# Down-projection weights as one 4 MB transfer per expert, gated values in groups of four columns

## What is computed

```
logits = xt @ w_router + b_router            # 32 experts, top 4 of them per token
gate   = softmax(top_val)
hu     = xb @ w_up[e] + b_up[e]              # 1024 -> 2048
x_glu  = min(hu[:, :1024], 7);  x_lin = clip(hu[:, 1024:], -7, 7)
act    = x_glu * sigmoid(1.702 * x_glu) * (x_lin + 1)
y      = act @ w_down[e] + b_down[e]         # 1024 -> 1024
out[token] += gate * y                       # then RMSNorm
```

## Time and profile before

| | us |
|---|---|
| median of 3 runs | 1251.53 |
| the three runs | 1251.39, 1251.53, 1255.16 |
| span of the profiled execution | 1248.5 |
| PE busy in it | 1169.1 (94%) |

### The profile page before, as it was taken

How to read it: one execution, slowest core, us unless ns; L and a number is a source line. 1 busy time by engine, 2 the same in 40 slices (tenths; PEclk the granted TensorE clock), 3 DMA queues, 4 the chain that set the end, 5 groups by cost and what they waited for, 6 DMA issues and landing times.

```text
span 1248.5 us, 17019 instructions
## 1 busy us (share of the span) xinstructions
PE 1169.1 (94%) x7215; PEld 604.2 (48%) x7216; DVE 445.6 (36%) x766; ACT 250.3 (20%) x353; POOL 15.9 (1%) x30
## 2 busy tenths in 40 slices
PE   9999999999999999899899989898989989899997
PEld 9998988888633343333333333333333333333332
DVE  5754546666532233222222222222322222222232
ACT  4544445544401010001000000000000001000012
POOL 2200000000000000000000000000000000000000
PEclk9999999999999999999999999999999999999999
DMA  9645333377999999999999999999999999999996
GB/s 296 219 169 186 135 135 135 135 277 282 371 417 425 431 431 427 430 430 429 431 433 427 431 430 429 430 430 434 433 428 431 433 427 431 435 427 432 421 428 278
DMA packets 50031, 456.98 MB, mean 366 GB/s; under 512 B 5988, under 2 KB 6136, under 8 KB 31400
## 3 DMA queue, kind: packets, MB, share of 16 engines
q1 hardware_dynamic: 49544, 455.09, 87.7%
q10 hardware_dynamic: 448, 1.32, 0.3%
HBM read 455.35 MB, written 1.05 MB: 366 GB/s over the span
## 4 chain that ended last, share of the span: by engine, by line
PE 59%; DMA 35%; DVE 2%; SPq 2%; ACT 1%; issue 1%; DVEq 0%
PE ps L1384 57%; DMA ring<-in_w_up_dram 22%; DMA arena<-in_w_up_dram 12%; PE ps L1891 1%; DMA ring<-in_w_in_dram 1%; ACT w_split L588 0%; SPq L397 0%; DVE w_split L892 0%; SPq L399 0%; PE ps L1777 0%; PE ps L1573 0%; SPq L414 0%; DVE arena L1062 0%; SPq L391 0%; PE ps L1680 0%
## 5 line engine op out<-in xcount | busy, mean ns | idle before, releaser
L1384 PE MATMUL ps<-ring,arena 128*64 128x512 f32 x2304 | 523.2, 608 | 50.9 <-DMA ring<-in_w_up_dram 50.9
L1384 PEld LDWEIGHTS ps<-ring,arena 128*64 128x64 f32 x2304 | 163.9, 140 | 378.8 <-issue 300.3
L1384 PE MATMUL ps<-arena 128*64 128x512 f32 (+3 forms) x920 | 202.7, 563 | 17.0 <-DMA arena<-in_w_up_dram 16.1
L1296 DVE TENSOR_SCALAR arena<-ps 128x512 f32<-128x512 f32 x32 | 22.1, 692 | 487.3 <-PE ps L1384 487.3
L892 DVE TENSOR_TENSOR w_split<-ring,w_split 128x2048 fp32r<-128x2048 f32 x48 | 109.8, 2291 | 108.4 <-ACT w_split L588 108.1
L1384 PEld LDWEIGHTS ps<-arena 128*64 128x64 f32 (+1 forms) x920 | 78.2, 149 | 128.4 <-issue 100.2
L796 ACT ACTIVATE arena<-arena 128x512 f32<-128x512 f32 x32 | 20.2, 631 | 552.6 <-DVE arena L1296 552.6
L1384 PE MATMUL ps<-w_split,x_split 128*128 128x512 f32 x528 | 123.5, 392 | 0.7 <-ACT arena L624 0.5
L1384 PEld LDWEIGHTS ps<-w_split,x_split 128*128 128x128 f32 x528 | 98.4, 188 | 21.8 <-issue 1.2
L588 ACT ACTIVATE w_split<-ring 128x2048 fp32r<-128x2048 f32 x47 | 89.6, 1911 | 70.7 <-PE ps L1384 62.5
L1384 PE MATMUL ps<-x_split,w_split 128*128 128x256 f32 x768 | 94.7, 284 | 0.1
(11 more groups left out here) (251 smaller groups left out, 624.8 us busy)
## 6 DMA issues: line engine op xcount, KB each, us to landing
ring<-in_w_up_dram SPq DMA_DIRECT2D x40, 4096.0 KB, 31.1
ring<-in_w_down_dram SPq DMA_DIRECT2D x46, 2048.0 KB, 30.2
arena<-in_w_up_dram SPq DMA_DIRECT2D x14, 4096.0 KB, 31.1
ring<-in_w_in_dram SPq DMA_DIRECT2D x17, 2048.0 KB, 7.8
arena<-in_w_down_dram SPq DMA_DIRECT2D x14, 2048.0 KB, 30.0
ring<-in_w_up_dram SPq DMA_DIRECT2D x12, 2048.0 KB, 23.1
arena<-in_w_up_dram SPq DMA_DIRECT2D x4, 2048.0 KB, 23.5
ring<-in_w_up_dram SPq DMA_DIRECT2D x8, 1024.0 KB, 8.7
```

Source lines behind the costliest of these rows:

```text
L1296: dve.tensor_scalar(glu_c, ps[bank][:, :], LIMIT, None, ALU.min).then_inc(glu_ok, 1)
L1384: return pe.matmul(dst, lhsT, rhs, start=start, stop=stop, skip_group_check=True)
```

## The change

The down weights of experts 1 to 30 are loaded as one 4 MB piece over a pair of places: partition p takes eight neighbouring rows, a run of 32 KB (`load_down_pair`). The piece waits for the second of the two places, and lands with one semaphore count. `down` waits for that count once, ahead of d = 0, where it waited for each half.

Place d of the pair now holds, on partition p, hidden rows 8p+4d to 8p+4d+3. The gated values must match, so the up matmuls and their bias read their 512 columns in groups of four, skipping every other group: half 0 takes columns 0-3, 8-11, 16-19, ..., half 1 the others (`hidden_half`). The count of matmuls, and every shape, stay. Expert 0 keeps the old columns and the old pieces. The last expert keeps its five pieces, with rows chosen to match.

```diff
-        def load_down(sp, e, d, n):
-            rows = w_down[0, bass.ds(e, 1), d * 512:d * 512 + 512, :]
-            sp.dma_start(chunk_at[n % PLACES], rows.rearrange("e (p s) n -> p (e s n)", s=4))\
+        def load_down_pair(sp, e, n):
+            rows = w_down[0, bass.ds(e, 1), :, :]
+            sp.dma_start(pair_at[n % PLACES // 2], rows.rearrange("e (p s) n -> p (e s n)", s=8))\
               .then_inc(chunk_in[n % PLACES], 16)
...
             def down_chunks(e, base, n):
-                for d in range(DOWN_CHUNKS):
-                    sp.wait_ge(chunk_used, base + (n + d - PLACES + 1))
-                    load_down(sp, e, d, n + d)
+                sp.wait_ge(chunk_used, base + (n + 1 - PLACES + 1))
+                load_down_pair(sp, e, n)
...
-                rows = w_down[0, E - 1, d * 512:d * 512 + 512, :].rearrange("(p s) n -> p s n", s=4)
+                rows = w_down[0, E - 1, :, :].rearrange("(p d s) n -> d p s n", d=DOWN_CHUNKS, s=4)[d]
...
+            def hidden_half(row, half):
+                return row.rearrange("p (q d s) -> p q d s", d=DOWN_CHUNKS, s=4)[:, :, half, :]
+
             def up_bias(m):
-                bias(0, m % UNROLL, 0)
-                bias(1, m % UNROLL, D)
+                for bank, first in ((0, 0), (1, D)):
+                    for half in range(2):
+                        mm(half_bank(bank, half), pickL[:, m % UNROLL, :], hidden_half(bias_p[:, first:first + D], half),
+                           True, False)
...
-                        col = (2 * s + side) * D + half * 512
-                        ins = mm(half_bank(banks[side], half), xin[:, m % 2, 2 * c + s, :], w[:, col:col + 512],
-                                 False, last_of_all)
+                        row = w[:, (2 * s + side) * D:(2 * s + side) * D + D]
+                        cols = row[:, half * 512:half * 512 + 512] if banks == FIRST_BANK else hidden_half(row, half)
+                        ins = mm(half_bank(banks[side], half), xin[:, m % 2, 2 * c + s, :], cols, False, last_of_all)
...
                 pe.wait_ge(actT_ok, i * UNROLL + (u + 1))
+                if not last:
+                    chunk_landed(i, first)
                 for d in range(DOWN_CHUNKS):
-                    def whole_landed():
-                        if d:
-                            odd_landed(i, first + d, last)
-                        else:
-                            chunk_landed(i, first)
-                    if not last:
-                        whole_landed()
```

More of the change, by code:

```diff
@@ L329, in layer @@
         pair_at = [at(G0, 2 * CHUNK)] + [ring[:, 2 * n:2 * n + 2, :].rearrange("p a n -> p (a n)") for n in range(3)]
-        ODD_LANDED = {1: 2, 3: 3, 5: 3, 7: 2}
         def load_up_pair(sp, e, c, n):
@@ L1793, in chunk_landed @@
                 pe.wait_ge(chunk_in[n % PLACES], i * (16 * TURN_CHUNKS // PLACES) + 16 * (n // PLACES + 1))
-            def odd_landed(i, n, last):
-                pe.wait_ge(chunk_in[n % PLACES], i * 16 + 16 * (ODD_LANDED[n % PLACES] + int(last)))
             def up_part(i, m, n, c, s, banks, last_of_all):
@@ L1876, in down @@
                             pe.wait_ge(early_in[2 + d], 32)
-                        if last and k == 2:
-                            whole_landed()
+                        if last and k == 2 and d == 0:
+                            chunk_landed(i, first)
+                        if last and k == 2 and d == 1:
+                            pe.wait_ge(chunk_in[PLACES - 1], 32)
                         if last and d == 1 and k == 3:
```

## The result

| | median | runs | profiled span | end of the last down matmuls |
|---|---|---|---|---|
| before | 1251.89 | 1250.60 to 1255.16 (6) | 1248.5 | 1239.44 |
| changed | 1254.83 | 1253.92 to 1257.12 (6) | 1252.7 | 1243.58 |

The ratio is 1.0028, 95% interval 1.0015 to 1.0041: the change costs 2.9 us by the medians, 4.2 us between the two profiled executions, where 1.5 us was forecast.

The account below looks back on a forecast made before the run. DMA was taken to bound the experts, with DMA and PE both critical at the end. Landings -3.3 us and the last turn's wait +4.8 us net +1.5 us on 1251.5, giving 1253.0, range 1249.5 to 1256.5.

Parts of the forecast that it names:

- Part 4: Down matmuls of experts 29 and 30: PE waits for one 4 MB landing instead of two, +4.8 us.
- Part 1: Down weights of 30 experts: runs of 32 KB instead of 16 KB bring landings 3.3 us earlier, 0.11 us per expert.
- Part 2: Up matmuls and their bias: reading columns in groups of four costs 0 us.
- Rival D: Up matmuls: the gaps slow them beyond PE's cover, 87 us over 30 experts, 1339; chance 4%.
- the factor 1.47: Up matmuls: far-end slowdown from gaps, taken from weight loads of one float per 16 bytes (209 against 142 ns).
- Part 3: Issue of the 4 MB piece, 3.4 us later, thinnest at expert 1: costs 0, bound 0 to 2 us.
- Rival C: Expert 1: the DMA queue runs dry for up to 2 us as the piece comes late, 1253 to 1255; chance 8%.
- A: Last turn: no late wait, so the gain of the longer runs comes through whole, 1248.2; chance 8%.
- B: Down weight loads: 32 KB runs bring nothing and the late wait stays, 1256.3; chance 10%.
- E: Down weight loads: each transfer has a fixed price and 30 fewer save it, 3.85 us; 1% for anything beyond.

Follow-up runs that it names:

- the second set: The changed kernel once more, unedited, against the kernel before (1250.73): 1254.76, ratio 1.003 (1.0020 to 1.0041).
- The first set of runs: The kernel before with both 2 MB down pieces issued when the later place is free, first measurement: 1252.93, ratio 1.0008 (0.9999 to 1.0018).

## Why the prediction was right, and where it was not

The median of 1254.83 lies inside the range of 1249.5 to 1256.5, 1.8 us above the forecast; the rise is 2.9 us instead of 1.5, and 4.0 us in the second set. Two pieces of luck made it look closer than it was. The base was the median of three runs, one of them at 1255.16, and was put 3.0 us above the profiled span, where every run on record lies 1.8 to 2.0 us above its own; that lifted the forecast by 1.1 us. And the six runs of before beside the first result have a median of 1251.89, 1.2 us above that of the 29 runs beside the second. In spans, which have neither, 1250.0 was forecast and 1252.7 and 1252.3 were measured.

**Part 4, the late wait: right, in place and size.** The step forecast a wait of 2.7 us at expert 29; the profile has 2.73, the second 1.70. Arrival and landing were both put 2.5 to 2.6 us too early (1192.9 and 1195.6 against 1195.53 and 1198.12), by the same wrong gain in landings, which cancels in their difference. The price of +4.8 us is 4.7 by undoing it and 4.6 (span) to 5.2 (medians) by adding it to the kernel before. The forecast wait of 1.8 us at expert 30 is 2.44 in one profile and 0 in the other; in the latter the lower clock used up that time. PE started 0.1 us after the landing in both, where 0.05 was taken, and the 16.04 us behind it were 16.04 again. Steady state stayed covered, by 0.5 us as said: PE starts the down matmuls of most experts 0.7 us after their landing, where it starts 0.1 us after it when it waits, and no wait for down weights shows elsewhere.

**Part 1, the gain of the runs: the term that was mis-sized.** Landings of expert 30 came 0.7 us earlier in the profiled pair (1227.45 against 1228.15), 1.1 in the second, not 3.3. By the version without the late wait the whole term is worth 0.7 us in the median. The step turned a gain in bytes per us into 0.11 us per expert and took 30 of them off every later landing. Two things were wrong with that. The gain per expert is 0.08 us (0.076 to 0.081 by the mean of the counts), which is 0.9 us less over 30. It lies within the bounds that the step gave (0.056 to 0.128), and their plain mean, 0.092, is nearer to it than the weight of three to one was. And PE waits for the last of sixteen counts, which the step let move with the rest. At expert 30's landing the mean came 1.9 us earlier in the changed kernel's profile and 2.0 us in the second, but the last hung 3.3 and 3.0 us behind it, against 2.1 us before: 1.2 and 0.9 us of the gain did not reach PE. The rest, 0.3 to 0.4 us, is mostly that both profiles were 0.2 to 0.3 us behind before's at 387 us already. Whether that larger lag of the last count belongs to the change or to these executions is open.

**Part 2, the groups: right.** 7.03 us as before, and 1.0002 alone. Rival D is out, and so is the factor 1.47: a matmul that reads four floats of every eight pays nothing here. This is what the Trainium skill has in "SBUF — State Buffer", "Door 1: The DMA port swizzle", for lines of 16 bytes, and the 7.03 us agree with it for a matmul's moving operand too. The row of 195 ns in the earlier trace rows mixes 16 loads from `h_sb` without gaps, 192 ns, with the 32 of the gather, 196 ns; by either reading two floats per 16 bytes cost 2 to 3%.

**Part 3, the later issue: right at 0.** Rival C's mechanism is refuted by the run that does it alone (447.15 against 447.10). A delay of its size is there, in its place, but in the last count alone, without the shift of the mean that a queue run dry would bring. The first set of runs, with its late start, would have passed for C's proof.

**Rivals.** A (no late wait, 1248.2) is refuted by the two waits. B (runs bring nothing, 1256.3) is nearer to the net than the forecast was, but not its mechanism: runs of 8 KB cost 4.2 us. E (a price per transfer) has nothing left to explain: the same run has before's number of transfers and pays 9 ns for each run that an engine has more, and at that price the 8 runs fewer per expert are worth 0.07 of the 0.08 us. The fixed 2.0 us that the Trainium skill has in "DMA: Bandwidth & Descriptors", "Anatomy of one DMA — SWDGE (gpsimd) path", is not seen between the transfers of this queue: 30 fewer, and the last landing moved by 0.7 us. **The sum** was +4.8 - 3.3 = +1.5; measured it is +4.7 - 0.7 = +4.0 in the second set of runs, which is 1254.76 - 1250.73.

## What to carry to other kernels

A larger transfer is a later first byte for its reader. Before merging pieces, list every place where the reader arrives between the two old landings: in the steady loop the slack may cover them (0.5 us did here), at the end of the stream nothing does, so keep the last pieces small. Where waits in a chain are held by one landing, removing an earlier one gives nothing, and can make the last wait long enough for TensorE's clock to drop (here 2.5 us on top); divide the last piece first. And a rate of bytes says where the mean of a landing's counts goes; the reader waits for the last, which here kept about 1 of 2 us from it.

## What was not expected of the hardware

- The granted clock fell to 1.2 GHz behind stands of PE of 2.73 and 2.82 us (matmuls behind them 8.78 us instead of 7.03), and during one of 4.72 us (6.18 instead of 3.65). Behind waits of 1.61, 1.70 and, at 1227.15, 2.44 us it did not (7.09, 7.09 and 3.65 us). The steady loop of before has the same: from 400 us on, 13 of its 34 rows behind a wait for up weights take 8.5 to 8.8 us, all behind 2.2 to 2.7 us, while the rows behind 2.41 and behind one of 2.63 us take 7.09. So the length of the stand alone does not decide it. In the steady loop the 1.7 us fit into the 3.7 us that PE has to spare per expert; at the end of the program a wait of 4.7 us took 7.2.
- A run costs each of the 16 engines about 10 ns beside its bytes. The page of the changed kernel counts 4320 packets fewer than before's (50031 to 45711), 480 of them under 512 B; the other 3840 are 128 per expert, 8 per engine if the sixteen share them evenly, so 0.08 us per expert is 10 ns a run. The kernel with 8 KB runs has 16 more per engine and expert and loses 0.145 us, 9 ns a run.
- The last of a landing's sixteen counts comes 0.7 to 3.7 us behind their mean in this full queue, and the distance grows in single steps: from 2.1 to 3.5 us between the landings of 545 and 565 us in the changed kernel, and from 1.3 to 1.8 and to 2.4 us at the same place in two profiles with the transfers of before. The cause is not known.
- Three of the profiled executions began the expert loop 3.9 to 4.4 us late, so what delayed them lies in the stages before the experts. It is not the change: one of the three has the pieces, runs and columns of before. The times of before hold single values of that distance too (1255.16 beside 1251.4), perhaps for the same reason.
